# Down projection: the loads of weight blocks for later products issued from ScalarE's queue

## The reference, cut to what matters

```python
    gate, val = jnp.split(conv, 2, axis=-1)
    y = (jax.nn.gelu(gate) * val) @ w_down      # (tokens, 2816) @ (2816, 1024)
    ...
    x = x + _rmsnorm(f, lw['g_ffn_post'])
```

## Time and profile before

| | us |
|---|---|
| median of 3 runs | 2545.74 (2541.14 to 2547.9) |
| the profiled execution, its own time | 2541.53 |
| its span in the profile | 2539.8 |
| TensorE busy | 2443.2 (96%) |
| VectorE busy | 1595.8 (63%) |
| ScalarE busy | 1100.1 (43%) |
| down projection: first to last product L3558 | 1813.6 to 2276 |

### The profile page before, as it was taken

One profiled execution on the slowest core, in us unless ns is written; L12 is line 12 of the kernel. 1 busy time (PEld: TensorE's weight loads), 2 busy tenths in 40 slices (PEclk: granted clock), 3 DMA queues, 4 the chain that ended last, 5 costly groups with the idle time before them and its releaser, 6 DMA issues. The chain is left out here.

```text
span 2539.8 us, 37994 instructions
## 1 busy us (share of the span) xinstructions
PE 2443.2 (96%) x13790; PEld 2197.3 (87%) x13790; DVE 1595.8 (63%) x2351; ACT 1100.1 (43%) x2005; POOL 743.4 (29%) x941
## 2 busy tenths in 40 slices
PE   8999999989999789999999999999799999989998
PEld 6788999977777689999999999999787788877887
DVE  4300232278887488889888898889646667763332
ACT  4311121144454356666566656666422323443332
POOL 1100000045565323344434455555200000112222
PEclk9999999989999899999999999999999999999999
DMA  5213778764344456564555545565559979972221
GB/s 176 92 59 113 237 225 269 222 177 134 119 130 130 139 175 196 175 188 134 189 184 188 160 144 177 176 207 179 161 152 296 286 193 303 296 249 104 82 74 46
DMA packets 467131, 440.59 MB, mean 173 GB/s; under 512 B 67539, under 2 KB 361235, under 8 KB 466937
## 3 DMA queue, kind: packets, MB, share of 16 engines
q1 hardware_dynamic: 466956, 438.34, 56.2%
HBM read 324.30 MB, written 113.95 MB: 173 GB/s over the span
## 5 line engine op out<-in xcount | busy, mean ns | idle before, releaser
L2679 PE MATMUL up_chain<-up_bh,up_ah 128*128 128x348 f32 (+1 forms) x1056 | 344.2, 326 | 19.8 <-DVE up_up L2531 10.6
L2679 PE MATMUL up_chain<-up_bh,up_al 128*128 128x348 f32 (+1 forms) x1056 | 342.4, 324 | 0.0
L2679 PE MATMUL up_chain<-up_bl,up_ah 128*128 128x348 f32 (+1 forms) x1056 | 342.2, 324 | 0.0
L2544 DVE SCALAR_TENSOR_TENSOR up_conv<-up_up,ffn_features,up_conv 128x696 f32<-128x696 f32 (+1 forms) x264 | 255.3, 967 | 59.6 <-ACT up_conv L2352 50.2
L3558 PE MATMUL down_acc<-down_bh,down_ah 128*128 128x512 f32 x616 | 243.1, 395 | 19.6 <-DVE down_bl L3310 11.2
L2223 POOL TENSOR_TENSOR up_conv<-up_conv 128x696 f32<-128x696 f32 (+1 forms) x66 | 131.7, 1995 | 412.9 <-DVE up_conv L2544 284.8
L2467 DVE TENSOR_TENSOR up_al<-up_sums,up_ah 128x512 fp32r<-128x512 f32 x256 | 239.1, 935 | 9.0 <-ACT up_ah L2284 9.0
L3558 PE MATMUL down_acc<-down_bh,down_al 128*128 128x512 f32 x616 | 241.4, 392 | 0.0
L3558 PE MATMUL down_acc<-down_bl,down_ah 128*128 128x512 f32 x616 | 241.3, 392 | 0.0
L2679 PEld LDWEIGHTS up_chain<-up_bh,up_ah 128*128 128x128 f32 x1056 | 201.6, 191 | 23.5 <-DVE up_up L2531 12.8
L2467 DVE TENSOR_TENSOR up_al<-up_raw,up_ah 128x512 fp32r<-128x512 f32 x192 | 185.5, 967 | 39.8 <-ACT up_ah L2284 39.8
(11 more groups left out here) (380 smaller groups left out, 6314.6 us busy)
## 6 DMA issues: line engine op xcount, KB each, us to landing
up_sums<-weight_sums SPq DMA_DIRECT2D x256, 256.0 KB, 3.9
up_raw<-in_w_up SPq DMA_DIRECT2D x64, 512.0 KB, 4.9
down_araw<-hidden SPq DMA_DIRECT2D x36, 704.0 KB, 6.9
in_up_raw<-in_w_up SPq DMA_DIRECT2D x44, 512.0 KB, 7.3
weight_sums<-in_up_sum SPq DMA_DIRECT2D x22, 1024.0 KB, 5.6
down_keep<-in_w_down SPq DMA_DIRECT2D x77, 256.0 KB, 5.8
up_raw<-in_w_up SPq DMA_DIRECT2D x64, 256.0 KB, 3.1
hidden<-up_conv SPq DMA_DIRECT2D x44, 348.0 KB, 3.6
```

The lines of the kernel that those rows point to most:

```text
L2544: last = nc.vector.scalar_tensor_tensor(out=out[:, 0:n], in0=up[g % 2][kind][:, c:c + n], in1=out[:, 0:n], scalar=taps[:, f, c:c + 1], op0 ...
L2679: last = nc.tensor.matmul(acc[:, 0:HALF[p]], a[:, q % RING, k, :], b[:, m - 1, k, left(p)], start=(opens and k == 0 and i == 0), stop=(k = ...
```

## The change

The loads of weights for walks after the first are issued by ScalarE in place of SyncE: in step `i` after `rounds(i + 2)` and before `round_w`. They wait for the same semaphores as before (the old block split, the temporary buffer summed). Loads of walk 1's weights, of features and of rows, and all stores stay on SyncE.

```diff
@block.sync
-            def load_b(v, k):
-                parts = B_PARTS[WALKS[v]]
-                if v > 0:
-                    sp.wait_ge(wready, chunk_at(v - 1, k) + 1)
-                    if WALKS[v - 1] == 6:
-                        sp.wait_ge(t2_stored, 16 * PAIRS)
-                sp.dma_start(keep[:, k, :], b_source(k, parts[0])).then_inc(keep_in[k], 16)
-                for part in parts[1:]:
-                    ...
-                    sp.dma_start(temps[n % 4], b_source(k, part)).then_inc(temp_in[n % 4], 16)
+            def load_b(k):
+                sp.dma_start(keep[:, k, :], b_source(k, B_PARTS[WALKS[0]][0])).then_inc(keep_in[k], 16)
...
             for k in range(DOWN_AHEAD, PAIRS):
-                load_b(0, k)
+                load_b(k)
...
                     load_step(i + 3)
-                if i + 1 < steps and walk_of(i + 1) == walk_of(i):
-                    for v, k in summed_at(i + 1):
-                        load_b(v, k)
                 for v, k in summed_at(i):
                     if WALKS[v] == 6:
                         store_t2(k)
...
@block.scalar
+            def load_b(v, k):
+                parts = B_PARTS[WALKS[v]]
+                if v > 0:
+                    act.wait_ge(wready, chunk_at(v - 1, k) + 1)
+                    if WALKS[v - 1] == 6:
+                        act.wait_ge(t2_stored, 16 * PAIRS)
+                act.dma_start(keep[:, k, :], b_source(k, parts[0])).then_inc(keep_in[k], 16)
+                for part in parts[1:]:
+                    n = B_TEMP_AT[v, k, part]
+                    if n < 4:
+                        act.wait_ge(tail_stored[n], 32 * len(range(n, groups, 4)))
+                    else:
+                        act.wait_ge(b_summed, n - 3)
+                    act.dma_start(temps[n % 4], b_source(k, part)).then_inc(temp_in[n % 4], 16)
...
                 if i + 2 < steps:
                     rounds(i + 2)
+                if i + 1 < steps and walk_of(i + 1) == walk_of(i):
+                    for v, k in summed_at(i + 1):
+                        load_b(v, k)
                 for v, k in split_at(i):
                     round_w(v, k)
```

## The result

The changed kernel took 2550.46 us (median of 9 runs, 2548.88 to 2552.53) against 2545.74 before: ratio 1.0025, 95% interval 1.0017 to 1.0034, that is 6.4 us more (4.3 to 8.7). The ratio goes by all runs of both kernels; the two medians alone lie only 4.7 us apart. The profiled execution took 2549.89, its span is 2548.2. Lines of the kernel have moved by 3: the products are L3561, the rests of features L3332, the sums of features L3324, the sums of weights L3308, the rests of weights L3313.

A forecast was written before the change was run, and what follows sets the result against it. TensorE was taken to bound the phase, with VectorE and its data close behind in walks 6 and 5. Gain 0 and price 2.9 + 2.2 = 5.1 us on 2545.7 gave 2551, range 2543 to 2562.

The forecast's parts named there:

- The gain of 0: Down projection: 121 issues leaving SyncE win 0, as DMA is full in walks 6 and 5; bound 3.9 us.
- not slower: Walks 6 and 5: SyncE's earlier feature loads bring data some 1.9 us sooner a pass; 2542 to 2546; chance 0.23.
- Walks 2, 7, 4 and 1 at nothing: Issues on ScalarE cost 0 in these four walks; without cover, 2.9 us a step for three steps of walk 2.
- 2.9 + 2.2 forecast: Price in us of walk 6 (middle of 1.9 to 3.8) and walk 5 (from 1.2 to 3.1), 5.1 together.
- the blocked case: ScalarE's issues wait behind SyncE's feature loads: price 10.2 us, or 13 (2559) with two low-clock stretches; chance 0.27.
- With four issues they begin at 1971.9, 1.9 late.: Walk 6, first pass: ScalarE's four issues delay the rounding of weights by 1.9 us, and VectorE's rests with it.
- its feature load went out 1.9 late: Walk 6, third pass: load waits for the first pass's late rests; 3.8 us in all if data is equally late, else 1.9.
- Blocked issues: Walk 6: ScalarE's issues must wait behind SyncE's feature load, 1.9 us more a pass on average; 2554 to 2566; chance 0.27.
- TensorE's waits in walks 6 and 5 were to rise to about 8: Sign in the changed profile: TensorE's waits for rests of features rise from 1.5 + 1.2 us to about 8.
- the weights' rounding was to start 1.9 us late and its waits to grow by 1.9 a pass: Sign in walk 6: rounding starts about 1.9 us after feature rounding; VectorE's waits for ScalarE grow some 1.9 a pass.

The follow-up runs named there:

- rounding first: Changed kernel with two ScalarE statements swapped, so that each step rounds the weights before issuing the loads; ratio 1.0034 to the kernel before.
- early: Changed kernel, but in walks 6, 7, 5 and 4 ScalarE issues the loads at the head of the step, before squares and feature rounding; ratio 1.0008 to the kernel before.
- after landing: Changed kernel, but in walks 6 and 5 ScalarE issues at the head of step i, once features of step i+2 have landed; ratio 1.0003 to the kernel before.

## Why the prediction was right, and what in it was not

**Time and direction.** 2551 was forecast, 2550.46 measured, the change slower by 0.25%, under what I counted as telling from no change. That the sum came so near is luck in part: the delay of which it was made measured less than half of what I took, and late data, which I had priced only as a consequence of that delay, made up for it.

**The gain of 0.** Right. SyncE, rid of the weights, stood waiting for the rests before its feature loads for 140.6 us, in place of 63.1:

```profile
SPq L3042 <- DVE down_al L3332: 140.6, 28, 9.4
```

So its feature loads went out as soon as a buffer was free, and still they landed later, not sooner: the *not slower* rival had its first half, earlier issues, and failed at the data. The Trainium skill's "DMA: Bandwidth & Descriptors", section "Issuing engines are not separate DMA queues", also says that transfers of several issuers interleave on the same DMA engines. The trace agrees: the feature load took 10.3 us to land with four of ScalarE's 256 KB loads under way beside it, 7.6 with hardly any bytes behind ScalarE's issues, and walk 6 moved no more GB/s with two queues (248) than with one (280).

**Walks 2, 7, 4 and 1 at nothing.** Right: the windows show TensorE full in walks 2, 7 and 4, walk 1 did not get longer, and the kernel with ScalarE's loads in these walks alone stands at 0.9993.

**Walks 6 and 5.** The place was right, the size too small: 2.9 + 2.2 forecast, 5.0 + 3.8 measured. Of the 5.0, 1.6 are the clock after a long wait, which I had priced for the blocked case alone. Of the 8.8, 0.5 came back in walk 1 and, in these two executions, 1.5 at the wait of walk 3 (2.99 in place of 4.49), which I had left alone and which varies by as much from kernel to kernel; 6.8 remain, and the ratio gives 6.4.

**The step that failed** is the one that makes the price: "With four issues they begin at 1971.9, 1.9 late." The issues overlap the rounding of features, and the weights' rounding began 0.56 to 0.76 us after it. VectorE's waits for it grew by 5.4 us over both walks, about 1 a pass, and where they were taken away alone (rounding first) nothing came back. What I had not priced is the data: I took the feature loads as late only by what their issue was late ("its feature load went out 1.9 late"), and the one followed here landed 1.7 us later from an issue that was on time, while weights issued after it on the other queue landed first. That the transfers on the second queue are needed for the loss is shown: same issues without bytes, no loss; same bytes issued late on one queue, no loss. In the changed kernel most of it is late data, along the chain 3.0 of 3.7 us in walk 6 and 3.7 of 3.8 in walk 5; later rounding has 0.7 and 0.1, net. How much taking away one of the two would give back is not settled: the chain closes over both, so that a microsecond taken from one wait turns up in part at another. With issues that spare the rounding (early) or the features (after landing), the waits added up to 29.9 and 30.0 us, against 36.1 and, before, 28.0.

**Blocked issues.** Refuted. The rival wanted first issues of 2 to 4 us on ScalarE behind SyncE's feature loads; in walks 6 and 5 ScalarE's took 0.33 to 0.64, one of them begun 0.32 us into an issue of SyncE that lasted 2.41. The rule of the Trainium skill on which it leaned ("Perfetto Trace Analysis", section "DMA Instruction — HWDGE (DVE, Sync)", one DMA at a time for two sequencers) did not show between SyncE and ScalarE; the measurement decides. SyncE's own issues stayed long (2.41 us) with the weights gone from its queue; what makes them long is not shown.

**What would have shown it.** TensorE's waits in walks 6 and 5 were to rise to about 8, and were 8.9; the weights' rounding was to start 1.9 us late and its waits to grow by 1.9 a pass, and both came out at half of that or less. The waits at the feature sums were not named as a sign of loss; they grew by 6.1 us and were the first thing to see.

No version with all its loads beats the kernel before for certain; the best leaves walks 6 and 5 on SyncE and has 0.9993 (0.9984 to 1.0001), clearly ahead of the changed kernel.

## What to carry to other kernels

One queue was also an order here: in walks 6 and 5 of the kernel before, loads landed in the order in which they were issued, and the urgent one stayed ahead. Before moving half of the loads to another engine's queue, find out which transfer a computing engine waits for, and whether DMA is full there; if both, the moved loads can make the one that matters land later, whatever the issues cost. And a wait that an experiment removes is worth what the chain gets back, not what the row says: add up all waits of the engine that sets the pace, before and after.

## What the runs showed of the hardware

- ScalarE issued DMAs while its own activation of 1.38 us ran (issues at 1979.81, 1980.19 and 1980.93, activation from 1979.75 to 1981.13), and while SyncE's issue of 2.41 us ran; these took 0.33 to 0.64 us each.
- Loads on two queues did not land in the order of their issue: 704 KB issued first landed after 10.3 us, at 1989.8; 4 x 256 KB issued up to 1.9 us later on another queue had all landed by 1987.8 (after 5.6 to 6.0 us in the median).
- Loads of 64 partitions in place of 128 moved half the bytes in 0.79 of the DMA time (22.1 to 27.9%), and their issues took longer (about 0.6 us in the median on ScalarE in walks 6 and 5, in place of 0.44). With such loads on SyncE's queue a feature load landed after 9.9 us in place of 8.6.
